# Splitting the first weight and input transfers into four pieces, and moving the constants behind them

## What is computed

```python
h = x @ w_in
c_q, c_kv, k_r, dq, dk, dv = jnp.split(h, splits, axis=-1)
lam = jnp.exp(jnp.sum(lp[0] * lp[1])) - jnp.exp(jnp.sum(lp[2] * lp[3])) + lambda_init
bias_dist = rel_bias.astype(jnp.float32)[t5_causal_bucket(jnp.arange(seq))]
# in diff_attention
bias = jnp.transpose(bias_dist[rel], (2, 0, 1))
logits = jnp.where(mask, logits + bias[None, :, None], -jnp.inf)
a = (p[:, :, 0] - lam * p[:, :, 1]).astype(v.dtype)
```

## Time and profile before

| | |
|---|---|
| median of the runs | 2111.26 us |
| span of the profiled execution | 2108.7 us |
| its device time apart from the span | not given; the span is 2.6 us under the median |
| TensorE busy | 2080.2 us, 99% |
| VectorE, ScalarE busy | 85%, 66% |
| first product of `in3` | 9.18 us |
| DMA in the first 42 us | 345 to 376 GB/s |

### The profile page before, as it was taken

How to read it: one execution, slowest core, us unless ns; L and a number is a source line. 1 busy time by engine, 2 the same in 40 slices (tenths; PEclk the granted TensorE clock), 3 DMA queues, 4 the chain that set the end, 5 groups by cost and what they waited for, 6 DMA issues and landing times. The chain is left out here.

```text
span 2108.7 us, 28117 instructions
## 1 busy us (share of the span) xinstructions
PE 2080.2 (99%) x11000; PEld 1759.1 (83%) x11000; DVE 1784.6 (85%) x2350; ACT 1399.8 (66%) x1845; POOL 58.6 (3%) x56
## 2 busy tenths in 40 slices
PE   8999999999999999999999999999999999999999
PEld 7878888878888888888888888879988888888887
DVE  5776768789999999999999999988878888878887
ACT  5555546568888888888888888857654545465544
POOL 0011002001000000000000000000000000000000
PEclk9999999999999999999999999999999999999999
DMA  9448664559999999999999999945446555336552
GB/s 310 163 138 270 222 217 150 207 185 396 393 396 395 394 396 388 380 376 391 369 393 372 385 383 379 394 174 157 144 151 228 181 198 159 103 110 230 180 196 104
DMA packets 284668, 567.07 MB, mean 269 GB/s; under 512 B 9180, under 2 KB 113760, under 8 KB 284288
## 3 DMA queue, kind: packets, MB, share of 16 engines
q1 hardware_dynamic: 277936, 538.31, 70.9%
q0 software_dynamic: 5728, 23.73, 3.1%
q10 hardware_dynamic: 864, 3.15, 0.4%
HBM read 556.23 MB, written 12.59 MB: 270 GB/s over the span
## 5 line engine op out<-in xcount | busy, mean ns | idle before, releaser
L444 DVE TENSOR_TENSOR wl<-raw,wh 128x1024 fp32r<-128x1024 f32 (+1 forms) x632 | 763.5, 1242 | 106.8 <-ACT wh L436 102.0
L436 ACT ACTIVATE wh<-raw 128x1024 fp32r<-128x1024 f32 (+1 forms) x632 | 647.1, 1053 | 165.8 <-PE psum L481 62.9
L444 DVE TENSOR_TENSOR wl<-arena,wh 128x1024 fp32r<-128x1024 f32 x384 | 456.8, 1222 | 37.9 <-ACT wh L436 32.7
L436 ACT ACTIVATE wh<-arena 128x1024 fp32r<-128x1024 f32 x384 | 403.8, 1062 | 85.0 <-PE psum L481 83.8
L479 PE MATMUL psum<-wh,xhl 128*128 128x512 f32 (+1 forms) x1136 | 449.3, 396 | 2.0 <-DVE wl L444 0.8
L481 PE MATMUL psum<-wh,xhl 128*128 128x512 f32 (+1 forms) x1136 | 441.5, 389 | 0.0
L480 PE MATMUL psum<-wl,xhl 128*128 128x512 f32 (+1 forms) x1136 | 440.6, 388 | 0.0
L471 PE MATMUL psum<-xhl,wh 128*128 128x512 f32 x980 | 349.4, 396 | 0.0
L479 PE MATMUL psum<-wh,yh 128*128 128x512 f32 x752 | 295.6, 393 | 1.0 <-DVE yl L1599 1.0
L481 PE MATMUL psum<-wh,yl 128*128 128x512 f32 x752 | 293.0, 390 | 0.0
L480 PE MATMUL psum<-wl,yh 128*128 128x512 f32 x752 | 292.6, 389 | 0.0
(11 more groups left out here) (440 smaller groups left out, 2083.5 us busy)
## 6 DMA issues: line engine op xcount, KB each, us to landing
arena<-in_moe_g SPq DMA_DIRECT2D x72, 1024.0 KB, 9.1
arena<-in_moe_u SPq DMA_DIRECT2D x72, 1024.0 KB, 8.8
raw<-in_moe_d SPq DMA_DIRECT2D x64, 1024.0 KB, 9.3
arena<-in_moe_d SPq DMA_DIRECT2D x48, 1024.0 KB, 9.1
raw<-in_ff_up SPq DMA_DIRECT2D x48, 1024.0 KB, 5.2
raw<-in_moe_g SPq DMA_DIRECT2D x40, 1024.0 KB, 7.9
raw<-in_moe_u SPq DMA_DIRECT2D x40, 1024.0 KB, 9.8
raw<-in_ff_down SPq DMA_DIRECT2D x24, 1024.0 KB, 5.7
```

The costliest lines, as they stand in the source:

```text
L436: A.activation(unit(s, i)[0], raw_half(s, i), ACT.Copy).then_inc(*s.w_hi.tick(i))
L444: V.tensor_tensor(lo, raw_half(s, i), hi.bitcast(F), SUB).then_inc(*s.w_lo.tick(i))
```

## The change

- Loads 0 and 1 (`in3`, `in4`) come in four pieces of 256 KB each, two row chunks of all 256 columns (`load_first`), each with a semaphore of its own; they are split by pieces of 128 x 512 (`hi_first`, `lo_first`), and multiplied by pieces (`first`): of each piece both halves of the columns, so that the two halves go to two banks. `in3` uses banks 0 and 1, `in4` banks 6 and 7; ScalarE's copies read from there.
- SyncE issues a piece of load 0 and a chunk of the input in turn, with the tables `oh` and `relb` behind the first chunk (48 KB and half a KB), then load 1 in pieces, load 2 whole, and only then the rest of `smalls` and of `consts` (two transfers).
- The product of `relb` and `oh` waits for these two tables alone. Lambda and the two products of the bias table go behind `in6`; on VectorE lambda's products go behind unit 10, its difference behind the table's addition; on ScalarE its exponential goes behind the copy of `in6`.

```diff
+    def load_first(m, c):
+        src, _, _, q, _, _ = main.w.loads[m]
+        Y.dma_start(RAW[:, q, :].rearrange("p (k x) -> p k x", k=8)[:, 2 * c:2 * c + 2, :], src[:, 2 * c:2 * c + 2, :]
+                    ).then_inc(*first_in[m][c].tick("all"))
+    def hi_first(m, c):
+        raw, hi, _ = first_piece(m, c)
+        A.wait_ge(*first_in[m][c].of("all"))
+        A.activation(hi, raw, ACT.Copy).then_inc(*main.w_hi.tick(("first", m, c), 2 * m, 2 * m + 1))
+    def lo_first(m, c):
+        raw, hi, lo = first_piece(m, c)
+        V.wait_ge(*main.w_hi.of(("first", m, c)))
+        V.tensor_tensor(lo, raw, hi.bitcast(F), SUB).then_inc(*main.w_lo.tick(("first", m, c), 2 * m, 2 * m + 1))
...
+        def first(m, b):
+            claim(b)
+            n = (3, 4)[m]
+            us = un[f"{st}.in{n}"]
+            for c in range(4):
+                T.wait_ge(*main.w_lo.of(("first", m, c)))
+                if m == 0:
+                    T.wait_ge(*dve.of(f"m0i.x{c}"))
+                for h, u in enumerate(us):
+                    w = unit(main, u)
+                    for k in (2 * c, 2 * c + 1):
+                        o, wh, wl = bk(2 * b + h)[:, 0:256], w[0][:, k, :], w[1][:, k, :]
...
         if l == 0:
             T.wait_ge(*x_in[0].of("all"))
             hold_clock(7, 2, XT[:, 0, 0:P], XT[:, 1, :])
-        proj(3, 0, by_chunks(("m0i", "f0ln")[l]))
-        empties(0, (act, f"{st}.dq0"))
+            first(0, 0)
+            drained(0, (act, f"{st}.dq0"))
...
+            T.wait_ge(*distances_in.of("all"))
+            T.matmul(take(4)[0:4, 0:384], S("relb")[0:32, :], C("oh")[0:32, :], start=True, stop=True
+                     ).then_inc(*pe.tick("bias.r4"))
+            empties(4, (dve, "bias.r4"))
+            first(1, 3)
+            drained(3, (act, f"{st}.dq1"))
...
+        proj(5, 2)
+        empties(2, (dve, f"{st}.dk0"))
+        proj(6, 3)
+        empties(3, (act, f"{st}.dk1"))
         if l == 0:
             T.wait_ge(*consts_in.of("all"))
             T.wait_ge(*smalls_in.of("all"))
...
+            lam()
             ps = claim(3)
             T.wait_ge(*tz_in.of("tz"))
             for n in range(2):
                 x = T.matmul(ps[:, n * 512:(n + 1) * 512], C("anti"), flat(CC[:, 2 * n:2 * n + 2, :]), start=True, stop=True)
```

More of the change, by code:

```diff
@@ L294, in program @@
     x_in = [sig(f"xT_landed{c}", 16) for c in range(4)]
+    first_in = [[sig(f"first{m}_landed{c}", 16) for c in range(4)] for m in range(2)]
+    distances_in = sig("distances_landed", 16)
     smalls_in, consts_in, pos_in = sig("smalls_landed", 16), sig("consts_landed", 16), sig("pos_landed", 16)
@@ L1006, in turn_heads, with lam @@
             x.then_inc(*pe.tick(name))
+        def first(m, b):
[10 more added lines that the diff above has]
+                        o, wh, wl = bk(2 * b + h)[:, 0:256], w[0][:, k, :], w[1][:, k, :]
+                        T.matmul(o, wh, XH[:, k, :], start=k == 0, stop=False)
+                        T.matmul(o, wh, XL[:, k, :], start=False, stop=False)
+                        i = T.matmul(o, wl, XH[:, k, :], start=False, stop=k == 7)
+                    if c == 3:
+                        i.then_inc(*pe.tick(("unit", u), f"{st}.in{n}"))
+        def lam():
+            T.wait_ge(*dve.of(f"{st}.lam"))
+            T.matmul(take(5)[:, 0:2], C("ones")[0:64, 0:128], LAM[0:64, 0:2], start=True, stop=True).then_inc(*pe.tick(f"{st}.lam"))
+            empties(5, (act, f"{st}.elam"))
         if l == 0:
@@ L1360, in latent, with lam, lam_done @@
                                        ).then_inc(*dve.tick(f"{st}.y{n}"))
[L1362 to L1367, removed]
+        def lam():
+            V.wait_ge(*smalls_in.of("all"))
+            V.tensor_tensor(LAM[0:64, 0:1], dl[0:64, 0:1], dl[0:64, 1:2], MUL).then_inc(*dve.tick())
+            V.tensor_tensor(LAM[0:64, 1:2], dl[0:64, 2:3], dl[0:64, 3:4], MUL).then_inc(*dve.tick(f"{st}.lam"))
+            V.tensor_scalar(DNL, S(f"dn{l}"), 1.0 - lam0, None, MUL).then_inc(*dve.tick(f"{st}.dnl"))
+        def lam_done():
+            V.wait_ge(*act.of(f"{st}.elam"))
+            V.tensor_tensor(LAM[:, 4:5], LAM[:, 3:4], LAM[:, 2:3], SUB).then_inc(*dve.tick())
+            V.wait_ge(*dve.last())
+            V.tensor_scalar(LAM[:, 4:5], LAM[:, 4:5], -lam0, None, ADD).then_inc(*dve.tick())
+        if l:
+            lam()
         lo_to(main, U + 4)
@@ L1372, in dve_mixer @@
         lo_to(main, U + 8)
[L1373 to L1376, removed]
+        if l:
+            lam_done()
         lo_to(main, U + 9)
@@ L1385, in dve_mixer @@
             V.wait_ge(*dve.last())
+        if l == 0:
+            lam_done()
         lo_to(main, U + 12)
@@ L3325, in scalar_program @@
     def scalar_program():
-        hi_to(main, 1)
         for c in range(4):
+            hi_first(0, c)
             A.wait_ge(*x_in[c].of("all"))
             act_x("m0i", c)
+        for c in range(4):
+            hi_first(1, c)
         act_mixer(0)
@@ L3370, in vector_program @@
     def vector_program():
-        lo_to(main, 1)
         for c in range(4):
+            lo_first(0, c)
             dve_x("m0i", c)
+        for c in range(4):
+            lo_first(1, c)
         dve_mixer(0, [(res_in, "all")])
@@ L3431, in sync_program @@
     def sync_program():
-        load_to(main, 1)
+        o, n = coff["oh"]
+        r, m = soff["relb"]
         for c in range(4):
+            load_first(0, c)
             Y.dma_start(XT[:, 2 * c:2 * c + 2, :], d["xT"][256 * c:256 * c + 256, :].rearrange("(k p) n -> p k n", p=P)
                         ).then_inc(*x_in[c].tick("all"))
-        Y.dma_start(SM[:, :], d["smalls"]).then_inc(*smalls_in.tick("all"))
-        load_to(main, 2)
-        Y.dma_start(CT[:, :], d["consts"]).then_inc(*consts_in.tick("all"))
+            if c == 0:
+                Y.dma_start(CT[0:32, o:o + n], d["consts"][0:32, o:o + n]).then_inc(*distances_in.tick())
+                Y.dma_start(SM[0:32, r:r + m], d["smalls"][0:32, r:r + m]).then_inc(*distances_in.tick("all"))
+        for c in range(4):
+            load_first(1, c)
+        load_to(main, 3)
+        Y.dma_start(SM[:, 0:r], d["smalls"][:, 0:r]).then_inc(*smalls_in.tick("all"))
+        Y.dma_start(CT[:, 0:o], d["consts"][:, 0:o]).then_inc(*consts_in.tick())
+        Y.dma_start(CT[:, o + n:cn], d["consts"][:, o + n:cn]).then_inc(*consts_in.tick("all"))
         load_to(main, 5)
```

35 lines of the change are left out of this document (29 added, 6 removed).

## The result

The change takes 2115.56 us, the median of 20 runs (2112.56 to 2116.73), against 2112.03 (2110.10 to 2114.03, 20 runs) for the kernel before, run beside it: a ratio of 1.0015, interval 1.0009 to 1.0021. By the ratio that is 3.2 us more (1.9 to 4.4; the two medians are 3.5 apart), where the forecast had 0.3 more. The time lies outside the range given, 2107.8 to 2114.2. The profiled execution took 2115.89 us with a span of 2114.1; here, 1.8 us lie around the span, where the prediction had reckoned 2.6.

What follows compares the result with a forecast made beforehand. TensorE, busy 99% of the span, was taken as the bound. Some 5.6 us won early were to be mostly waited away: -0.5 plus 0.8 for the clock gave +0.3 us, so 2111.6 us, range 2107.8 to 2114.2.

Steps and rivals of the forecast that it cites:

- What bounds the kernel: TensorE, busy 99% of the span; gains or losses by the first products of block 4 (in0) should reach the end.
- Start in four pieces: At the start: first input chunk at 4.8 instead of 6.88 us, 2.1 us sooner; first product at about 7.1.
- Constants and read-back: TensorE's waits for constants (1.3 us before the distance product) and for the table read back (2.0 us) go.
- Blocks: Weight loads of 1024 KB, 0 (in3) to 6 (in2): block 2 lands at 14.7, block 3 near 22.7; in6 ends at 31.7.
- The new wait: Lambda's product behind in6 waits for VectorE's split of block 5, landing at 34.2; TensorE stands still 5.0 us from 31.7.
- The clock term: Behind that pause TensorE runs at a lower clock: 0.8 us lost, the middle of bounds 0 and 1.7.
- The sum: Whole kernel: -0.5 + 0.8 = +0.3 us, so 2111.6 us.
- the wait does not bind: Faster rival: block 5 comes by 29 us, all 5.6 us stay won, 2105.7 us; chance 0.09.
- the pieces cost the queue: Slower rival: nine more transfers at 520 ns each land block 5 4.7 us later, 2116.3 us; chance 0.07.

Runs made afterwards that it cites:

- lambda early: The change with lambda's two VectorE products moved ahead of the split of unit 8, TensorE's order kept; 2109.02 us, ratio 0.9990 to the kernel before.
- input late: The change with the input X (1024 KB) issued behind blocks 5 and 6 instead of ahead of block 5; 2111.67 us, ratio 0.9998 to before.
- held: The change with nine unused products put between in6 and lambda on TensorE, to keep it busy; 2110.96 us, ratio 1.0004 to before.
- pieces only: The kernel before with only loads 0 and 1 and the input in pieces; tables, distance product and lambda in their old places; 2113.07 us, ratio 1.0011.
- tables later: "lambda early" with the two small tables issued behind the third input chunk instead of the first; 2108.24 us, ratio 0.9982 to before.
- all together: "tables later" with block 3 issued ahead of smalls and consts, and X behind blocks 5 and 6; 2105.60 us, ratio 0.9970 to before.

## Why the prediction was wrong

**What bounds the kernel: right.** The edits acted in the first 45 us: +3.2 us at the first logits, +3.2 in the ratio. That these agree to a tenth is in part luck, since in the other kernels the two differ by up to 2.3 us.

**Start in four pieces: right in kind, too low in size.** Forecast 2.1 us; the chunk came 2.4 us sooner and the first product at 6.00 instead of 9.18, 3.2 sooner. The latter is better because VectorE splits the input behind a piece of 0.69 us now, where half a block of 1.23 us stood ahead of it. But the first 14 products ran at 0.21 us, not 8, and one waited 0.34 us for the split input, so the distance product stood at 14.13 with its end at 14.86, where 14.4 was forecast for the latter.

**Constants and read-back: right.** Both waits are gone. The table landed at 30.7, not 28.5, which is still ahead of TensorE.

**Blocks: 2 and 3 missed.** Block 2 was forecast at 14.7 and landed at 17.0, still in time; block 3 was forecast at 22.7 and landed at 25.1. The prediction let the queue run at the pace of before from the first input chunk on (2.8 us per unit), and it moved 289 GB/s up to 10 us instead of 368. TensorE waited 0.8 us for block 3 and ended `in6` at 33.3, not 31.7. As the prediction said, the lambda wait hid the slip. With lambda early it is no longer hidden.

**The new wait: right.** Forecast 5.0 us and lambda at 36.7; measured 4.3 us and 37.7. Block 5 landed 0.9 us later than taken (35.1 for 34.2, at the upper bound); lambda followed. It was issued at 21.3, 2.2 us sooner than before and not "some 5 us": block 2, late itself, was split by 20.5, and SyncE stood in the issue of `X` from 17.76 to 21.3. "Lambda early" and "input late" show that this wait is where the gain went: take it away and 4.2 us are won at the logits instead of 3.2 lost.

**The clock term: the step that failed.** The prediction took 0.8 us, with bounds of 0 and 1.7. From the lambda product to the logits were 7.8 us; at full clock the same work takes 5.1 ("lambda early", "held"), so the term is 2.7 us. The middle was taken in the hope that part of the slow time would fall into the pause, of which 0.9 of 6.8 us did. The upper bound came from the rows of one execution behind a 3.2 us wait and was read as the most there could be, although the pause that was forecast was longer. That same wait stands in every kernel here, at a place that no edit touched (L763 before, L788 with the change). The same 24 products behind it, from "pieces only", from the change and from "tables later":

```profile
1410.91 2.83 PE L788 MATMUL psum<-consts,smalls 128*128 128x128 f32 x24 [2.77 <-DVE SC L2445]
```

```profile
1412.88 4.21 PE L788 MATMUL psum<-consts,smalls 128*128 128x128 f32 x24 [2.77 <-DVE SC L2451]
```

```profile
1406.23 5.38 PE L788 MATMUL psum<-consts,smalls 128*128 128x128 f32 x24 [3.01 <-DVE SC L2452]
```

By the stretches around it, the time at the low clock was nothing in two of the ten profiled executions (pauses of 2.77 and 2.79 us), 3.4 us in five (2.77 to 3.16, before among them) and 6.8 us in three (3.01 to 3.30). So the row that gave 1.7 us was one outcome of several: the same place can cost 3.4 us of full-speed work, and a longer pause is more often followed by the larger price, with no fixed tie. The Trainium skill, "TensorE: Matmul & The Clock Gate", Part 1, says that an idle array is set back to 1.2 GHz until it has been busy again; the trace agrees (0.50 in 38 to 42 us). The 1.7 us that the prediction would have paid by it stood nearer to the outcome than the middle that I chose, but under it too.

**The sum.** -0.5 forecast for the shift; block 5 and what follows it 1.0 later makes +0.5; the clock's 2.7 makes +3.2. Had the clock term stood at 2.7, the sum would have been 2113.5, inside the range, and with block 5 at its upper bound as well the chance for slower by over 0.2% could not have stayed at 0.08. The range did have both unknowns at their bad ends together (0.4 lost and 1.7 make its 2.1); it was missed mainly because the clock's end was too low. With 2.7 in its place and the same margin the range would end at 2115.2, 0.4 under the measured median, and the rest is that the kernel before, run beside the change, took 0.8 us more than the 2111.26 that the sum starts from.

**The rivals.** That the wait does not bind was wrong, as given. That the pieces cost the queue 0.43 us each or more was wrong: "pieces only" has block 5 where it was before, and blocks 2 and 3 only 0.7 us later. The rival's price, issue time per transfer, did show up at one place, the two small tables. The 2.0 us per transfer that the prediction takes from the Trainium skill, "DMA: Bandwidth & Descriptors", stand there ("Anatomy of one DMA") for transfers that GpSimd issues, and the pieces come from SyncE; no run here shows them laid end to end. The ratio came out on the slower side by another way than this rival.

**What is open still.** Why block 3 lands 1.5 to 2.5 us later in the kernels with pieces and the new order than with whole loads; two parts of it are measured above, their cause is not. And why single executions of one kernel differ by up to 6 us. A part of that is the clock at places that no edit touched: the 0, 3.4 or 6.8 us at the low level around L763, and in some profiled executions two more stretches of 3.4 us near 1815 and 1836 us, where TensorE waits 0.6 us at most (the change has both, before has neither). Each 3.4 us costs 1.7. That is of the order of the whole effect here, and it may be why 4.2 us at the logits come out as 2.1 in the median of "lambda early"; it also means that the 2.7 us of the clock term are those of one profiled execution, and need not be the same in each of the 20 runs.

## What to carry to other kernels

When a change starts an engine sooner, look for what the engine's own order makes it wait for next, and move that first: here three VectorE instructions of 0.15 us, which needed nothing of the block ahead of them, decided between 3.2 us lost and 2.1 won. Price a pause of TensorE with the slow products behind it, and take the upper bound of that price from several executions, with pauses at least as long as the one forecast: a single row here showed half of what the same wait can cost. If the pause cannot be avoided, products that nothing uses keep the clock and save the second part.

## What was not expected of the hardware

- The low clock behind a pause was not proportional to it, nor the same each time. In the profiled executions, pauses of 1.6, 2.0 and 2.3 us left no stretch below 1.00, those of 2.8 to 3.3 us at one and the same place came with 0, 3.4 or 6.8 us at 1.2 GHz, and those of 4.2 and 4.3 us with 6.8 us each. A start that is sooner can so make the whole longer.
- A transfer of half a KB took SyncE 0.42 us to issue, one of 256 KB 0.47. Between pieces it takes as much of SyncE's time as a piece: 289 GB/s from 3 to 10 us with the tables behind the first chunk, 320 and 313 behind the third ("tables later", "all together"), 346 with pieces and no small table among them. With a whole load issued first, the tables at their place behind the first chunk left 347 and 349.
